# Query projection in two 512-column pairs, gate products between tiles, heads of the last pair one tile at a time

## The reference, cut to what matters

```
kv = (rmsnorm(h, kv_norm) @ kv_w).reshape(B, T, N_BRANCH, 2, N_KV_HEADS, HEAD_DIM)
...
proj = xn @ w_in
q = proj[..., :N_HEADS * HEAD_DIM].reshape(B, T, N_KV_HEADS, Q_PER_KV, HEAD_DIM)
gates = jax.nn.sigmoid(proj[..., N_HEADS * HEAD_DIM:].astype(jnp.float32)).reshape(...)
q_n = rmsnorm(q, q_norm)
o_cmp, o_slc, o_win = branches(q_n, rope(q_n, pos))
```

## Time and profile before

| what | us |
|---|---|
| median of three runs | 1545.93 (1545.2 to 1548.83) |
| the profiled execution's own time | 1547.87 |
| its span, first to last instruction | 1546.1 |
| TensorE busy | 1510.3 (98%) |
| VectorE busy | 1051.8 (68%) |
| ScalarE busy | 637.3 (41%) |
| mean granted TensorE clock | 0.998 of full speed |

### The profile page before, as it was taken

The page is one execution under the profiler, slowest core; times in us unless marked ns, Lnnn a source line. Parts: engine busy times, 40 slices in busy tenths (PEclk is TensorE's granted clock), DMA queues, the critical chain, the costliest instruction groups (busy, mean ns, idle before and its releaser), DMA issues.

```text
span 1546.1 us, 29268 instructions
## 1 busy us (share of the span) xinstructions
PE 1510.3 (98%) x11968; PEld 1394.4 (90%) x11968; DVE 1051.8 (68%) x1559; ACT 637.3 (41%) x1064; POOL 94.5 (6%) x155
## 2 busy tenths in 40 slices
PE   7999999999999999999999998998999999999998
PEld 5779999999999999998789766776799999999998
DVE  4438753358877869756266787877667969678952
ACT  5325221234333324334334667676543424334422
POOL 0000000000000000000000124554000000000000
PEclk9999999999999999999999999999999999999999
DMA  5348222322232323232325503104542222323232
GB/s 169 123 141 273 84 85 75 102 87 82 69 107 71 123 82 99 80 109 82 109 77 154 164 27 138 56 2 137 139 120 90 77 95 81 111 69 123 78 103 69
DMA packets 129866, 157.12 MB, mean 102 GB/s; under 512 B 11930, under 2 KB 106482, under 8 KB 129330
## 3 DMA queue, kind: packets, MB, share of 16 engines
q1 hardware_dynamic: 129394, 155.29, 31.6%
q10 hardware_dynamic: 352, 0.15, 0.0%
HBM read 149.58 MB, written 14.16 MB: 106 GB/s over the span
## 4 chain that ended last, share of the span: by engine, by line
PE 89%; DVE 7%; ACT 2%; issue 1%; DMA 1%; POOL 0%; SPq 0%; DVEq 0%; ACTq 0%
PE PS L758 40%; PE PS L1092 21%; PE PS L831 9%; PE PS L1393 2%; PE PS L1408 2%; PE PS L1310 2%; PE PS L790 1%; PE PS L1365 1%; PE PS L1273 1%; DVE wl L2157 1%; PE PS L841 1%; PE PS L1029 1%; PE PS L1376 1%; PE PS L1528 0%; PE PS L1471 0%
## 5 line engine op out<-in xcount | busy, mean ns | idle before, releaser
L2157 DVE TENSOR_TENSOR wl<-raw,wh 128x2048 fp32r<-128x2048 f32 (+2 forms) x89 | 167.9, 1886 | 127.8 <-ACT wh L1668 83.2
L1643 ACT ACTIVATE wh<-raw 128x2048 fp32r<-128x2048 f32 (+2 forms) x75 | 114.3, 1524 | 227.0 <-PE PS L758 140.2
L2214 DVE TENSOR_TENSOR hT<-PS,hT 128x544 f32<-128x544 f32 (+1 forms) x104 | 75.1, 722 | 130.7 <-PE PS L758 130.3
L1092 PE MATMUL PS<-opL,whA 128*128 128x272 f32 x512 | 148.5, 290 | 0.0
L1092 PE MATMUL PS<-opH,whA 128*128 128x272 f32 x512 | 147.7, 289 | 0.3 <-DVE wlB L2478 0.3
L1092 PE MATMUL PS<-opH,wlA 128*128 128x272 f32 x512 | 147.7, 288 | 0.0
L758 PE MATMUL PS<-act0h,wh 128*128 128x272 f32 x640 | 133.3, 289 | 0.4 <-DVE sg L2370 0.4
L758 PE MATMUL PS<-act0l,wh 128*128 128x272 f32 x640 | 132.2, 288 | 0.0
L758 PE MATMUL PS<-act0h,wl 128*128 128x272 f32 x640 | 132.1, 288 | 0.0
L1092 PE MATMUL PS<-opL,whB 128*128 128x272 f32 x384 | 111.4, 290 | 0.0
L1092 PE MATMUL PS<-opH,wlB 128*128 128x272 f32 x384 | 110.7, 288 | 0.0
(11 more groups left out here) (418 smaller groups left out, 3754.8 us busy)
## 6 DMA issues: line engine op xcount, KB each, us to landing
raw<-in_ffn_w_gate SPq DMA_DIRECT2D x44, 512.0 KB
raw<-in_ffn_w_up SPq DMA_DIRECT2D x44, 512.0 KB
raw<-in_a_w_in SPq DMA_DIRECT2D x32, 512.0 KB, 4.7
raw<-in_ffn_w_down SPq DMA_DIRECT2D x64, 256.0 KB
raw<-in_a_w_out SPq DMA_DIRECT2D x16, 512.0 KB
crows<-in_cache_kv_cmp SPq DMA_DIRECT2D x32, 256.0 KB, 3.0
cache<-in_state_kv_win SPq DMA_DIRECT2D x8, 1024.0 KB, 7.5
out_kv_win_sample<-in_state_kv_win SPq DMA_DIRECT2D x8, 1016.0 KB
```

Source lines behind the costliest of these rows:

```text
L1092: mm = pe.matmul(PS[:, bank, 0:HALF], w, X[:, x, k, :], start=(k == 0 and not last and X is opH), stop=(k == 3 and last))
L1643: act.activation(wh[:, rs, 0:kn, :], raw[:, rs, 0:kn, :], ACT.Copy).then_inc(w_hi, 1)
L2157: dve.tensor_tensor(wl[:, rs, 0:kn, :], raw[:, rs, 0:kn, :], wh[:, rs, 0:kn, :].bitcast(F32), ALU.subtract).then_inc(w_ready, 1)
L2214: dve.tensor_tensor(h, psum_u(s, mt), h, ALU.add).then_inc(free[s], 1)
```

## The change

Items 0 to 3 of the queries become two pairs of `pair_b`, numbers 3 and 4 behind the key/value projection's 0 to 2, with the same round of six banks. `item_b`, `query_evac` and the narrow few products are dropped. In the last pair `between` puts three pieces between tiles: the gate products after tile 1 of the first half, the gates' transposes after tile 3 of the first half, the gate rows after tile 1 of the second half. ScalarE stores, squares and takes roots in the order 0, 1, 2, QT, 3 (LATE_TILES): pair 3 as one group of five tiles for root and heads, pair 4 a tile at a time. The gates' sigmoid is followed by a reload of the root table. On VectorE the first split (item 2 of the queries) moves between the two branches' key rotations; the copies of the keys' turns move behind the heads. TensorE waits for k_done tile by tile. The banks of the 15 turns are dealt out anew.

```
-    at_q = plan.take(4, 4)
+    at_q = plan.take(4, 0)
...
-    TURN_BANK = (0, 1, 2, 3, 4, 5, 0, 1, 2, 3, 4, 5, 2, 3, 4)
-    TURN_FREED_BY = (None,) * 6 + (0, 1, 2, 3, 4, 5, 8, 9, 10)
+    TURN_BANK = (2, 4, 5, 3, 0, 1, 2, 4, 5, 3, 2, 4, 5, 3, 2)
+    TURN_FREED_BY = (None,) * 6 + (0, 1, 2, 3, 6, 7, 8, 9, 10)
...
+    LATE_TILES = (0, 1, 2, QT, 3)
+    QUERY_READY = (3, 4, 5, 7, 7)
... SyncE
-        segment_few(at_q, b_w_in[0], 0, 14, 0, 4)
+        segment_wide(at_q, b_w_in[0], 0, 14, 0, 4)
...
-        sp.wait_ge(halves, 2 * (at_q[1] + 4))
+        sp.wait_ge(wide_mm, Q_LAST + QT)
... TensorE
+        for w in range(3, 5):
+            pair_b(w, at_kv, (act1, few_q, part_b, sel_b), 8, V_TILES, 4,
+                   between={(0, 1): gate_products, (0, 3): gate_turns, (1, 1): gate_rows} if w == 4 else {})
...
+            if n in (1, 2, 4, 5):
+                pe.wait_ge(wide_free, Q_LAST + (None, 1, 2, None, 3, 4)[n])
+            elif n == 3:
+                pe.wait_ge(g_d, 1)
...
-        pe.wait_ge(k_done, 3)
         for t in range(TT):
+            pe.wait_ge(k_done, QUERY_READY[t])
             turn_queries(t, 1, t_bank(TK + TT + t))
... ScalarE
+        wide_split(0, at_q[0] + 2, wide_done, 15)
+        for t in LATE_TILES:
+            query_stored(0, t)
+            query_squared(0, t)
+        wide_split(1, at_q[0] + 3, wide_mm, Q_LAST)
+        wide_partials(part_b, 18)
+        query_root(2, slice(0, 40))
+        act.wait_ge(gate_mm, 1)
...
+        root_table()
+        for j, t in enumerate(LATE_TILES):
+            query_stored(1, t)
+            query_squared(1, t)
+            query_root(3 + j, slice(8 * t, 8 * t + 8))
+        take(TK)
+        take(TK + 2)
... VectorE
+        wide_partials(part_b, 16)
...
             if br == 0:
-                partials(part_b, 1, 15)
+                split(0, at_q[0] + 2)
...
+        split(1, at_q[0] + 3)
+        wide_partials(part_b, 18)
+        dve.wait_ge(k_sq, 7)
+        query_means(slice(0, TT), 2)
+        query_heads(0, slice(0, TT), 2)
+        for j, t in enumerate(LATE_TILES):
+            one = slice(t, t + 1)
+            dve.wait_ge(k_sq, 8 + j)
+            query_means(one, 3 + j)
+            if j == 2:
+                dve.wait_ge(g_sel, 1)
+                link(dve.tensor_tensor(gtmp[:, :, :, :], PS[:, 3, 0:48 * (NB // 2)]...
+                dve.tensor_reduce(gd[:, :, :], ...).then_inc(g_d, 1)
+            if j == 4:
+                for half in range(2):
+                    link.put(dve.memset(rowsP[half][:, NG, :], 0.0))
+                take(0)
+            query_heads(1, one, 3 + j)
+        for n in range(1, TK):
+            take(n)
+        take(TK + 1)
         take(TK + 3)
```

More of the change, by code:

```diff
@@ L236, in build_program @@
     ksqt = at("ksqt", A_P0 + 22528, [P, TT, 512])
[L237 removed]
+    qsqt = at("qsqt", A_V + 13312, [P, TT, 2 * CW])
     gwh = at("gwh", A_V + 24576, [P, KT, 3 * NH], F32R)
@@ L781, in item_a, with pair_b @@
                         mid()
[L783 to L824, removed]
+        def pair_b(w, at, X, f0, i0, p0, first=None, mid=None, few_ready=None, between={}):
             (xh, xl), few, part, sel = X
@@ L867, in pair_b @@
                         mm = tile(t, k)
+                    if t < QT - 1 and (0, t) in between:
+                        between[0, t]()
             else:
@@ L880, in pair_b @@
                     mm = tile(t, k)
-                if t == QT - 1 and first is not None:
-                    mm = gather()
                 mm.then_inc(wide_mm, 1)
-                if t == QT - 2 and first is None:
-                    gather()
+                if t == (QT - 2 if first is None else QT - 1):
+                    gather().then_inc(wide_done, 1)
+                if (1, t) in between:
+                    between[1, t]()
         def segment(item, at, turns, X, kn=KT, fresh=None, mid=None):
@@ L1169, in _, with gate_products @@
         pe.wait_ge(f_ready, 3)
[L1170 to L1185, removed]
+        def gate_products():
+            pe.wait_ge(gw_lo, 1)
+            pe.wait_ge(wide_free, Q_LAST)
+            for k in range(KT):
+                for W, Xp, last in ((gwh, act1[0], False), (gwh, act1[1], False), (gwl, act1[0], True)):
+                    for h in range(2):
+                        mm = pe.matmul(PS[0:3 * NH, 2 + h, 0:HALF], W[:, k, :],
+                                       Xp[:, k * T + h * HALF:k * T + h * HALF + HALF],
+                                       start=(k == 0 and W is gwh and Xp is act1[0]), stop=(k == KT - 1 and last))
+            mm.then_inc(gate_mm, 1)
@@ new lines, in gate_turns, with gate_rows @@
+        def gate_turns():
+            pe.wait_ge(gate_st, 2)
+            for t in range(TT):
+                m = P if t < QT else TD
+                tr = pe.transpose(PS[0:m, 2, t * 48:t * 48 + 48], gT[:, t * P:t * P + m], ident[0:3 * NH, 0:3 * NH])
+            tr.then_inc(gate_tr, 1)
+        def gate_rows():
+            pe.wait_ge(s_late, 16 * 6)
+            pe.wait_ge(gate_done, 2)
+            for bp in range(NB // 2):
+                mm = pe.matmul(PS[:, 3, 48 * bp:48 * bp + 48], late[0:TD, C_SEL + bp * P:C_SEL + (bp + 1) * P],
+                               gates[0:TD, QT, :], start=True, stop=True)
+            mm.then_inc(g_sel, 1)
@@ L1234, in _ @@
         tr.then_inc(c_tr, 1)
[L1236 to L1241, removed]
         pe.wait_ge(s_pos, 16 * 8)
         for j in range(2):
-            tr = pe.transpose(PS[:, 7, j * SUB:j * SUB + SUB], posr[:, j, :], ident[0:SUB, 0:SUB])
+            tr = pe.transpose(PS[:, 6, j * SUB:j * SUB + SUB], posr[:, j, :], ident[0:SUB, 0:SUB])
         tr.then_inc(c_ss, 1)
-        pe.wait_ge(k_done, 3)
         for t in range(TT):
+            pe.wait_ge(k_done, QUERY_READY[t])
             turn_queries(t, 1, t_bank(TK + TT + t))
@@ L1934, in _ @@
+        wide_split(0, at_q[0] + 2, wide_done, 15)
[6 more added lines that the diff above has]
+        act.wait_ge(gate_mm, 1)
+        for h in range(2):
+            act.activation(gT[:, h * HALF:h * HALF + HALF], PS[0:3 * NH, 2 + h, 0:HALF], ACT.Copy).then_inc(gate_st, 1)
         act.wait_ge(gate_tr, 1)
@@ L2613, in _ @@
         for br in range(2):
-            heads(key(br), 20 * br, 1 + br)
+            heads(key(br), stats[:, 20 * br:20 * br + 20], 1 + br, TT, NG)
+        wide_partials(part_b, 16)
         for br in range(2):
```

149 lines of the change are left out of this document (52 added, 97 removed).

## The result

The changed kernel takes 1550.81 us as a median of seven runs, the kernel before, beside it, 1547.69: the ratio is 1.0024, with a 95% interval of 1.0015 to 1.0034. The change costs about 3.7 us (2.3 to 5.3). That is less than the 0.3% which the prediction took for what can be told apart, but the whole interval lies on the slower side, and 1550.8 lies above the range (1542.4 to 1548.8). The kernel before scatters by more than its first three runs showed: in three later series its medians are 1547.75 to 1547.84, its runs 1545.1 to 1550.1. One slow execution in the series of x4 (3797.86 us) and one of the kernel before beside x9 and x10 (1653.76) enter no ratio.

The account below looks back on a forecast made before the run. TensorE was taken to bound the query round and VectorE's queue the stretch behind it; compression products starting 0.6 us sooner gave 1547.87 - 0.6 = 1547.3 profiled, about 1545.3 as a median (profile 1.9 above it), range 1542.4 to 1548.8.

Parts of the forecast that it names:

- The round: Query products: 1.15 us less for wide products, 0.6 less waiting, 1.3 added for gates; about 56.8 us instead of 57.2.
- the wait for the split: TensorE's 0.6 us wait before item 2 for VectorE's split goes; the split ends at about 808, cover 2.5 us.
- the refills: In the round, some refills at 0.1 us around the gate pieces add 0.0 to 0.3 us.
- VectorE's queue: Behind the round VectorE's summed work sets the pace; first compression product at about 856.6 instead of 857.2, 0.6 us sooner.
- I scale from 1280 columns: VectorE's 512-column steps by proportion: 1.49 x 0.4 = 0.6 us; per tile 0.8 for means, 1.55 for heads.
- From here VectorE never rests: From tile 2's heads at 843.9, VectorE works without idling to 856.5, TensorE's turns fitting in.
- I take the same loss after: Low clock costs as before, about 1.5 us under the first compression products; unknown from -1.5 to +3.4 us.
- Rival 3: Gaps before turns 6 and 7 drop the clock at about 849; start 0.7 us later, up to +4.1; 1546.6 to 1550; chance 0.2.
- the prediction's own signs of being wrong: Behind the round: VectorE idle over 2 us, distance under 11 or over 16, clock full or down over 10; elsewhere 1 us moved.
- Rival 1: Tail behind the round folds up: compression products start at 851.0, 6 us sooner; 1538 to 1540 us; chance 0.08.
- Rival 2: Behind the round the clock stays up, VectorE slightly quicker: -2 to -3 us, 1543 to 1544; chance 0.17.
- Rival 4: In the round the pair's split comes late, VectorE 2.5 us later than worked out: +1 to +2 us; chance 0.03.

Follow-up runs that it names:

- x4: Changed kernel with the five key turns and VectorE's copies of them put between the tiles of the last pair; ratio to the kernel before 1.0006.
- x9: Changed kernel with keys turned in the round, some query copies earlier (TK+2 ahead of ScalarE's last root), first compression rows on ScalarE; 1546.76 us, ratio 0.9995.
- x10: Changed kernel with key copies ahead of the last two tiles' heads, first query turn in bank 6, work shifted to ScalarE; ratio to before 1.0004.
- x1: Changed kernel with ten filler products (float32, 256 columns) in TensorE's gaps behind the round; ratio to the kernel before 1.0017.
- x5: Kernel before with six filler products (float32, 256 columns) in TensorE's four gaps behind its round; ratio to the kernel before 1.0005.
- x2: Changed kernel with VectorE's five copies of the turned keys moved ahead of the last two tiles' heads; ratio to the kernel before 1.0008.
- x8: Changed kernel again, unaltered, as a second series; ratio to the kernel before 1.0025.

## Why the prediction was wrong, by its steps

**The round: right in its parts, one term too small.** Wide products do cost 0.232 us each, the wait for the split is gone (TensorE 57.22 busy of 57.22), the split came at 808.4, and the gates caused no wait. But the round is 57.2 us, not 56.8 (nor 57.05, the upper end of the sum). The gate rows cost 1.02 us to the next start rather than 0.9, and the refills, put at 0 to 0.3, are more: pair 4's products take 30.54 - 5.93 - 0.41 - 1.02 - 0.47 = 22.71 us where 96 x 0.2317 = 22.24 was reckoned, 0.47 more, and pair 3's 22.43, 0.19 more. So nothing was left of the 0.5 us that the round was to bring, and VectorE's queue, which starts with the squares of each tile, starts later by as much.

**VectorE's queue: the steps that failed are its start, "I scale from 1280 columns" and "From here VectorE never rests".** The first compression product was to start at 856.6. With the clock held up (x1, 1.18 us added to its times, so that its round starts at 785.88 too) it starts at 858.5, 1.9 us later. VectorE in x1:

```profile
840.26 0.69 DVE L2565 TENSOR_REDUCE stats<-qsqt 128x8 f32<-128x512 f32 x1 [0.99 <-ACT qsqt L1880]
...
849.15 0.69 DVE L2539 TENSOR_TENSOR qtok<-qtok,hgain 128x512 f32<-128x512 f32 x1
...
853.54 0.26 DVE L2634 COPY rowsP<-PS 128x16 f32<-128x16 f32 x2 [0.37 <-PE PS L1212]
854.12 0.69 DVE L2604 COPY qTn<-PS 128x512 f32<-128x512 f32 x1 [0.33 <-PE PS L1190]
```

- The sums of tile 2 start at 841.4 instead of 840.7. ScalarE can take the tile only at 840.05, where TensorE was to be through at 839.4, and the square takes 0.63 us, not 0.5.
- The last heads end at 851.0 instead of 850.0. A 512-column step was put at 0.6 us; the trace shows 0.69, and 0.72 from start to start, so a tile takes 0.89 and 1.69 where 0.8 and 1.55 were put. Only 0.3 us of this add to the 0.7, as the walk had some reserve.
- From there to the compression product it takes 7.4 us, not 6.6: VectorE does rest, 0.37 and 0.33 us, for TensorE's turns, which were to fit in.

With 1.49 us at 1280 and 2.82 at 2560 columns the three durations lie on one line: 1.04 ns a column and 0.16 us for each instruction. The Trainium skill, "VectorE: DVE Perf Modes", section "The TRN2 errata", says that VectorE's operations that read SBUF are slower by a fixed cost for each instruction, and not by a factor; its formula for a float32 tensor_tensor, (N + 151) / 0.96 ns, gives 691 ns at 512 columns and 1491 at 1280. The trace agrees (0.69 and 1.49 us), and either would have given a better size than the proportion.

The sign fell with the queue already: with the clock held up in both kernels the change costs 1.23 us, where 0.6 us of gain were forecast.

**The clock: "I take the same loss after" failed as well.** In the traced executions the loss went from 1.47 to 2.64 us (1.8 in the second profile), in a place where it delays the start of the products. Rival 3 had the mechanism, the place (the gaps before turns 6 and 7), the time of the fall (849; measured 850.6) and the sign, with a chance of 0.2. It was undersized at the start (0.7 us; the distance grew by 3.9), since I let the half speed begin only with the cache transposes at 852. In fact the three turns ahead of them, 12 transposes in 2.53 us, were slow as well and started at 852.20, over a us late by the queue. Queue and clock were priced each by itself; they add, as late copies both lengthen the gaps and put more turns into the slow time. That its total of up to +4.1 us holds the measured 2.4 to 3.7 is luck: most of that total was to be low clock under the products, and there the clock was up again at 860.8, before the first of them. Its times, 1546.6 to 1550, don't hold 1550.8.

Three of the prediction's own signs of being wrong came: behind the round VectorE is idle for 4.0 of 18.0 us (over 2), the distance is over 16 us, and the clock is down for 10.2 us (over 10).

**The others.** Rival 1 (the tail folds up) is out: the lower end was VectorE's queue, as argued; x1, x5 and x2 all end in a wait for VectorE's last copy (1.52, 0.93 and 1.5 us). Rival 2 (clock kept up) didn't occur, and x1 shows what it would have been: still 1.2 us worse than before with its clock up. Rival 4 fell: the split had 2.6 us in hand. For rival 3 the prediction quoted the Trainium skill, "TensorE: Matmul & The Clock Gate", section "Part 4: PE-mode transpose", that transposes don't count as TensorE being busy in the same way; the runs bear this out only in part. Transposes with gaps ran for 7 us at full clock after, and ten before, and what kept the clock up in x1 and x5 was the same gaps filled with products. No run filled them with transposes.

**The centre and the range.** The forecast was put beside the median of three runs, 1545.93; 24 and 33 later runs of the same kernel give 1547.8. Nearly 2 us of the miss in the absolute time come from that, and the range had no room for it. Moved up by as much it would still end below 1550.8. As a difference: forecast -0.6 us, measured about +3.7 by the ratio and +2.4 by the stretch, or +2.9 by the span, in the first pair of traces (+1.6 by the stretch of x8).

## What to carry to other kernels

When a stretch is bound by one engine's queue, take work out of that queue or reorder it before work is taken off another engine: here only the order of VectorE's copies was worth some 2.5 us of the ratio's 3.7 (x2 against the changed kernel, 1.0008 against 1.0024; the ends of the intervals just overlap). Cutting instructions finer hides them under products and pays a fixed cost for each; price it by a line through two sizes, not by proportion. And where TensorE is left with transposes and gaps (the longest ahead of the fall of the clock was 1.02 us in the kernel before, 2.41 after), price the clock together with the wait, not as an even chance both ways. Last, a stretch read from one execution needs the scatter of the kernel beside it.

## What was not expected of the hardware

- The clock falls once behind the round in each of the ten profiles without filler, but its place moves by several us between two executions of one program (down from 850.6 to 860.8, and from 848.5 to 855.4), and in x9 it came after a gap of 2.26 us, when TensorE was at work again. Its cost depends on the work it lies under: 1.5 us under compression products, 1.8 and 2.6 under the turns.
- In the second profile of the changed kernel the clock came back from 0.66 (854 to 856) to 1.00 (856 to 858) while TensorE did transposes only: it came back without a product between them.
- Six products in the gaps of the kernel before held the clock at 1.00, and the stretch became 1.47 us shorter, yet the time didn't: the ratio is 1.0005.
- The runs of the kernel before lie in two groups, near 1546 and near 1548.5. Of 35 at a mean clock of 0.999, 23 lie in the first, of 40 at 0.998 only 9, which fits a fall of the clock that only some executions have. But 12 at 0.999 lie in the second group, so the clock isn't all of it; their traces weren't taken, and the cause stays open.
